# Values of the first attention branch made for four heads at a time, and a later place for the other branches' values

## The reference

```python
for l in range(2):
    h, hc = modulated rmsnorm of x, of ctx
    p = h @ w_in ; pc = hc @ w_in[:, :KV_COLS]      # latents, keys, values, queries, gates
    # branch 1 ("mla"): 8 heads, keys and values out of a latent of 256 features
    kv_m = (rmsnorm(ckv) * w) @ mla_w_ukv            # per head: 64 key, 64 value columns
    q_m  = (rmsnorm(cq) * w) @ mla_w_uq              # per head: 96 columns
    o_m  = softmax(q_m k_m^T * scale) v_m            # 512 queries on 768 keys
    # branch 2 ("swa"): window of 128 tokens and the context; branch 3 ("ax"): dense
    o_s, o_a likewise with k_s, v_s, k_a, v_a straight out of p
    x += gate * (sum over branches of sigmoid(g) * ((o * silu(z)) @ w_o)) @ w_out
    # in layer 0 the context takes the same way as queries; in layer 1 it doesn't
```

## Time and profile before

| | us |
|---|---|
| runs: median, lowest, highest | 1783.66, 1782.36, 1784.66 |
| span of the profiled execution | 1785.1 |
| TensorE busy | 1711.1 (96%) |
| VectorE busy | 1084.0 (61%) |
| ScalarE busy | 1049.3 (59%) |
| GpSimd busy | 528.0 (30%) |

### The profile page before, as it was taken

How to read it: one execution, slowest core, us unless ns; L and a number is a source line. 1 busy time by engine, 2 the same in 40 slices (tenths; PEclk the granted TensorE clock), 3 DMA queues, 4 the chain that set the end, 5 groups by cost and what they waited for, 6 DMA issues and landing times.

```text
span 1785.1 us, 27001 instructions
## 1 busy us (share of the span) xinstructions
PE 1711.1 (96%) x10554; PEld 1498.7 (84%) x10554; DVE 1084.0 (61%) x2185; ACT 1049.3 (59%) x1921; POOL 528.0 (30%) x300
## 2 busy tenths in 40 slices
PE   7999999999999999999999999999999999999997
PEld 3777888889989889899889996788888887888787
DVE  5543776765565566665775655477775756565634
ACT  3433778766666777666321253577776677786322
POOL 1523123222232212212322353322333432332442
PEclk9997999999999999999999999899999999999999
DMA  9111102111121111111644331111212221212642
GB/s 326 40 37 28 26 24 55 27 42 48 42 60 43 47 37 36 42 48 36 201 153 166 118 97 49 40 34 37 60 48 66 72 64 44 60 49 65 200 142 95
DMA packets 178527, 129.53 MB, mean 73 GB/s; under 512 B 21661, under 2 KB 167647, under 8 KB 178400
## 3 DMA queue, kind: packets, MB, share of 16 engines
q1 hardware_dynamic: 174242, 115.37, 22.7%
q10 hardware_dynamic: 2878, 8.24, 1.3%
q0 software_dynamic: 1280, 4.20, 0.7%
HBM read 123.58 MB, written 4.19 MB: 72 GB/s over the span
## 4 chain that ended last, share of the span: by engine, by line
PE 76%; DVE 10%; ACT 7%; issue 3%; POOL 2%; DMA 1%; SPq 0%; DVEq 0%; ACTq 0%; POOLq 0%
PE acc L1357 56%; PE wide L1415 6%; PE ptp L1435 6%; PE pv L1448 4%; PE pv L1449 3%; DVE nmax L1991 2%; ACT e L1682 2%; DVE pt L2016 1%; DMA w_raw<-in_ada_w 1%; POOL h_lo L1844 1%; DVE k_m L1552 1%; ACT w_hi L1600 1%; DVE k_s L1552 1%; DVE q_s L1552 1%; POOL w_lo L1806 1%
## 5 line engine op out<-in xcount | busy, mean ns | idle before, releaser
L1806 POOL TENSOR_TENSOR w_lo<-w_raw,w_hi 128x1024 fp32r<-128x1024 f32 (+2 forms) x192 | 392.0, 2045 | 1085.0 <-ACT w_hi L1600 1084.8
L1357 PE MATMUL acc<-h_hi,w_hi 128*128 128x512 f32 (+2 forms) x1320 | 463.3, 352 | 10.3 <-DVE cq_lo L1554 3.9
L1357 PE MATMUL acc<-h_hi,w_lo 128*128 128x512 f32 (+2 forms) x1320 | 462.0, 351 | 0.0
L1357 PE MATMUL acc<-h_lo,w_hi 128*128 128x512 f32 (+2 forms) x1320 | 457.7, 350 | 0.3 <-POOL h_lo L1844 0.3
L1991 DVE TENSOR_REDUCE nmax<-wide 128x1 f32<-128x768 f32 (+3 forms) x240 | 189.6, 790 | 167.9 <-PE wide L1415 166.2
L1357 PEld LDWEIGHTS acc<-h_hi,w_hi 128*128 128x128 f32 (+1 forms) x1320 | 248.4, 188 | 50.1 <-issue 7.9
L1697 ACT ACTIVATE pt<-ptp 128x512 fp32r<-128x512 f32 (+3 forms) x312 | 165.8, 563 | 210.4 <-PE ptp L1435 208.6
L1357 PEld LDWEIGHTS acc<-h_hi,w_lo 128*128 128x128 f32 (+1 forms) x1320 | 248.2, 188 | 33.4
L1357 PEld LDWEIGHTS acc<-h_lo,w_hi 128*128 128x128 f32 (+1 forms) x1320 | 246.1, 188 | 34.2 <-POOL h_lo L1844 0.5
L1689 ACT ACTIVATE e<-e,einv 128x768 f32<-128x768 f32 (+3 forms) x240 | 193.5, 806 | 70.2 <-DVE einv L2008 69.8
L2016 DVE TENSOR_TENSOR pt<-ptp,pt 128x512 fp32r<-128x512 f32 (+3 forms) x312 | 191.8, 640 | 43.9 <-ACT pt L1697 43.7
(11 more groups left out here) (216 smaller groups left out, 3103.1 us busy)
## 6 DMA issues: line engine op xcount, KB each, us to landing
w_raw<-in_w_in SPq DMA_DIRECT2D x102, 512.0 KB, 3.9
w_raw<-in_ada_w SPq DMA_DIRECT2D x48, 512.0 KB, 5.3
w_raw<-in_w_out SPq DMA_DIRECT2D x16, 512.0 KB, 4.2
w_raw<-in_w_in SPq DMA_DIRECT2D x16, 256.0 KB, 3.3
w_raw<-in_w_o_mla SPq DMA_DIRECT2D x16, 256.0 KB, 2.8
w_raw<-in_w_o_swa SPq DMA_DIRECT2D x16, 256.0 KB, 2.8
w_raw<-in_w_o_ax SPq DMA_DIRECT2D x16, 256.0 KB, 2.9
w_raw<-in_mla_w_uq SPq DMA_DIRECT2D x16, 144.0 KB, 2.4
```

The costliest lines, as they stand in the source:

```text
L1357: ins = nc.tensor.matmul(dst, lhs, rhs, start=first, stop=last)
L1806: nc.gpsimd.tensor_tensor(w_lo[s][:, 0:k], w_raw[s][:, 0:k], f(w_hi[s][:, 0:k]), ALU.subtract).then_inc(w_lo_ready, 1)
```

## The change

It does five things. `mla_head` makes values for four heads at once, at heads 0 and 4: three groups of two token tiles, each tile six matmuls with 256 moving columns. `v_m` becomes three separate places, used by pair number modulo three; the third lies at 12288 to 18432, in the first half of `v_s`. The chunks change with it: "mk" holds key columns of two heads and either value columns of four heads or the query columns of one; "mq" can hold the queries of two heads. An eviction of values is two pieces, one for each pair. And `values_a` may run only when the output of head 5 has been issued, which a new entry in `issued` tells; it also stands behind `values_b` in the queue now.

```diff
@@ attention, loop
                 O(turned)
+                if turned["closes"]:
+                    issued["o", turned["branch"], turned["h"]] = n["s"]
@@ mla_head
             if h % 2 == 0:
-                c = chunk("mk", l, h, h + 1 if h else 0)
+                four, heads = h % 4 == 0, (0, 1) if h == 0 else (h + 1,)
+                cq = chunk("mq", l, heads) if h == 0 else None
+                c = chunk("mk", l, h, None if four else h + 1)
...
-                vg = [group("vm", chunk_ids=(c,), mode="vm", l=l, cost=cost_of(128, 6 * 3), co=KKV * 2 * MLA_NOPE,
-                            tts=range(tt, tt + 3), what="vm", pair=h // 2, needs=lambda: latents) for tt in range(0, TT, 3)]
-                ready_v["mla", h // 2] = vg
-                qg = head_q(h + 1 if h else 0, c, KKV * 2 * (MLA_NOPE + MLA_V))
-            if h == 0 or h % 2 and h + 1 < HEADS:
-                qg += head_q(h + 1, chunk("mq", l, h + 1), 0)
-            if h % 2 == 0 and h:
-                return [s for g in (kg[0], vg[0], kg[1], vg[1], *qg) for s in g["steps"]]
-            return [s for g in qg + kg + vg for s in g["steps"]]
+                if four:
+                    vg = [group("vm", chunk_ids=(c,), mode="vm", l=l, cost=cost_of(256, 4 * 3), co=KKV * 2 * MLA_NOPE,
+                                tts=range(tt, tt + 2), what="vm", pair=h // 2, needs=lambda: latents) for tt in range(0, TT, 2)]
+                    ready_v["mla", h // 2] = ready_v["mla", h // 2 + 1] = vg
+                    cq = chunk("mq", l, heads) if cq is None else cq
+                    for i, hq in enumerate(heads):
+                        qg += head_q(hq, cq, i * KQ * MLA_K)
+                else:
+                    qg = head_q(h + 1, c, KKV * 2 * MLA_NOPE)
+            elif h + 1 < HEADS:
+                qg += head_q(h + 1, chunk("mq", l, (h + 1,)), 0)
+            if h == 0:
+                return [s for g in qg + kg + vg for s in g["steps"]]
+            if h % 4 == 0:
+                return [s for g in (kg[0], vg[0], kg[1], *vg[1:], *qg) for s in g["steps"]]
+            return [s for g in kg + qg for s in g["steps"]]
@@ queue
-        item("values_a", "mla", cost_of(256, 72), lambda s: ("mla", 1 + len(tgs)) in s, values_s(0))
         z_item(0, 3)
         item("values_b", "mla", cost_of(256, 72), lambda s: ("mla", 5) in s, values_s(TT // 2))
+        item("values_a", "mla", cost_of(256, 72), lambda s: ("o", "mla", 5) in s, values_s(0))
@@ memory
-    v_m = shared("v_m", [P, 2, TT, 2, 2, HD], R, 75776)
+    v_m = [shared(f"v_m{i}", [P, TT, 2, 2, HD], R, at) for i, at in enumerate((75776, 81920, 12288))]
@@ matmuls, mode "vm"
-                        c0 = g["co"] + k * 2 * MLA_V
-                        wv = [w[s][:, c0:c0 + 2 * MLA_V] for w in (w_hi, w_lo)]
+                        c0 = g["co"] + k * 4 * MLA_V
+                        wv = [w[s][:, c0:c0 + 4 * MLA_V] for w in (w_hi, w_lo)]
...
-                    run(a[:, i * 2 * HD:(i + 1) * 2 * HD], pairs)
+                    run(a[:, i * 4 * HD:(i + 1) * 4 * HD], pairs)
@@ pieces
+            if what == "vm":
...
+                for i in range(2):
+                    v = v_m[(g["pair"] + i) % 3][:, t0:t1]
+                    out_.append((v[:, :, :, 0, :], v[:, :, :, 1, :], got[:, :, 2 * i:2 * i + 2, :]))
```

More of the change, by code:

```diff
@@ L793, in schedule @@
             if h % 2 == 0:
-                cost += cost_of(SEQ, 6) + cost_of(CTX, 6) + 2 * cost_of(128, 18)
+                cost += cost_of(SEQ, 6) + cost_of(CTX, 6)
+            if h % 4 == 0:
+                cost += 3 * cost_of(256, 12)
             item(("mla", h), "mla", cost, lambda s, h=h: h < 2 or ("mla", h - 2) in s, lambda h=h: mla_head(h), urgent=True)
@@ L1094, in chunk_dma @@
                 got, at = [], 0
[L1095 to L1100, removed]
-                               t_in["mla_w_uq"][l, :, hq * MLA_K:(hq + 1) * MLA_K].rearrange("(k p) c -> p k c", p=P))]
+                for a, many in ((0, 2), (1, 4 if hq is None else 0)):
+                    for k in range(KKV if many else 0):
+                        rows = t_in["mla_w_ukv"][l, k * P:(k + 1) * P, h * P:(h + many) * P].rearrange("p (h a d) -> p h a d", h=many, a=2)
+                        got.append((raw[:, at:at + many * HD].rearrange("p (h d) -> p h d", h=many), rows[:, :, a, :]))
+                        at += many * HD
+                if hq is not None:
+                    got.append((raw[:, at:at + KQ * MLA_K].rearrange("p (k c) -> p k c", k=KQ),
+                                t_in["mla_w_uq"][l, :, hq * MLA_K:(hq + 1) * MLA_K].rearrange("(k p) c -> p k c", p=P)))
+                return got
             if kind == "mq":
-                hq = chunks[c][2]
-                return [(raw[:, 0:KQ * MLA_K].rearrange("p (k c) -> p k c", k=KQ),
-                         t_in["mla_w_uq"][l, :, hq * MLA_K:(hq + 1) * MLA_K].rearrange("(k p) c -> p k c", p=P))]
+                return [(raw[:, i * KQ * MLA_K:(i + 1) * KQ * MLA_K].rearrange("p (k c) -> p k c", k=KQ),
+                         t_in["mla_w_uq"][l, :, hq * MLA_K:(hq + 1) * MLA_K].rearrange("(k p) c -> p k c", p=P)) for i, hq in enumerate(chunks[c][2])]
             b, t = chunks[c][2:]
@@ L1115, in chunk_size @@
             if kind == "mk":
-                return KKV * 2 * (MLA_NOPE + MLA_V) + KQ * MLA_K
+                return KKV * 2 * MLA_NOPE + (KKV * 4 * MLA_V if chunks[c][3] is None else KQ * MLA_K)
             if kind == "mq":
-                return KQ * MLA_K
+                return len(chunks[c][2]) * KQ * MLA_K
             return KO * P if kind == "wo" else CHUNK
@@ L1192, in v_of @@
             if pa["branch"] == "mla":
-                v = v_m[:, (pa["h"] // 2) % 2, kt, pa["h"] % 2, :, :]
+                v = v_m[pa["h"] // 2 % 3][:, kt, pa["h"] % 2, :, :]
             else:
@@ L1526, in pieces @@
                 return out_ if only is None else out_[only:only + 1], w
-            if what in ("vs", "vm"):
+            if what == "vs":
                 t0, t1 = g["tts"][0], g["tts"][-1] + 1
-                heads = 2 * KVH if what == "vs" else 2
-                v = v_s[:, t0:t1] if what == "vs" else v_m[:, g["pair"] % 2, t0:t1]
-                got = src[:, 0:(t1 - t0) * heads * HD].rearrange("p (t g d) -> p t g d", g=heads, d=HD)
+                v = v_s[:, t0:t1]
+                got = src[:, 0:(t1 - t0) * 2 * KVH * HD].rearrange("p (t g d) -> p t g d", g=2 * KVH, d=HD)
                 return [(v[:, :, :, 0, :], v[:, :, :, 1, :], got)], None
+            if what == "vm":
+                t0, t1 = g["tts"][0], g["tts"][-1] + 1
+                got = src[:, 0:(t1 - t0) * 4 * HD].rearrange("p (t g d) -> p t g d", g=4, d=HD)
+                out_ = []
+                for i in range(2):
+                    v = v_m[(g["pair"] + i) % 3][:, t0:t1]
+                    out_.append((v[:, :, :, 0, :], v[:, :, :, 1, :], got[:, :, 2 * i:2 * i + 2, :]))
+                return out_, None
             raise KeyError(what)
```

## The result

The changed kernel takes 1799.45 us (median of 4 runs, 1797.22 to 1803.38), 1.0098 times the time before [1.0074, 1.0121]. Run again beside the kernel before it gave 1.0094 [1.0063, 1.0126]. It is **some 17 us slower**; forecast were 1778.8 us and a range to 1791. The profiled execution took 1798.48 us with a span of 1796.4.

The account below looks back on a forecast made before the run. The prediction took TensorE, busy for 96% of the span, to bound the kernel. Its terms, -15.4 - 5 - 1.8 + 18 - 3.7 + 3 = -4.9 us, taken off the median 1783.66, gave 1778.8 us, range 1766 to 1791.

Parts of the forecast that it names:

- The sign that the prediction had named: Prediction is wrong if branch 1's attentions, 196 and 162 us long before, are together shorter by over 10 us or longer at all.
- Term 1: Inside branch 1's attentions: 216 narrow value matmuls become 72 with 256 columns, 15.4 us less.
- Term 4: Units left without filling, mainly heads 4 and 5 of both layers, as values_a waits: 18 us more, bounds 9 and 24.
- Term 3: First filling of layer 1: the wait for the low part of its weights goes, 1.8 us less.
- Term 5: Heads 6 and 7: moved values thicken the filling and shrink the stops there, 3.7 us less, between 0 and 6.
- Term 6: Behind heads 4 and 5: two falls of the clock of 3.4 us, 3 us more, bounds 0 and 19.
- Term 2: 72 value matmuls ahead of the attentions: the low clock lasts shorter in each layer, 5 us less, bounds 0 and 7.8.
- the one on the clock: Rival: clock falls and stays down in heads 4 and 5, +18 or 19 us instead of +3, 1795 us; chance 0.16.

## Why the prediction was wrong

The sign that the prediction had named came true: branch 1's attentions are together 17.7 us longer, where it had allowed none. And heads 4 and 5 have six short falls of the clock, where it had allowed two.

**The premise failed first**: "what leaves TensorE's row of work shortens the kernel", read from 96% busy. Busy time says that TensorE works, not that it decides. Term 1's price per matmul was about right (0.108 and 0.118 us between starts over all rows at full clock), its sum of 15.4 us worked out rightly, and with everything else held in place the same amount brought nothing (+2.5 us [-0.9, +5.9]): 12.4 of the 15.8 us came back as stops. The prediction booked nothing against Term 1 itself. It booked stops in Term 4, nearly all of them for units that are left quite bare, and only 2.6 us for units that keep one step of filling.

**The step that is missing** is the wait for an accumulator: 9.8 us in the trace, 7 us in the runs by taking it out, 8 us by putting it in. The prediction listed what the moved groups compute and what they cost, and did not ask what they had separated. The values between the two key groups gave the evictions time; the earlier trace rows even had the first trace of it, 2.4 us of idle behind `k_m` in front of the values.

**Terms 3, 4 and 5** forecast 18 - 1.8 - 3.7 = 12.5 us more stops, pipeline included. TensorE's idle time in the attentions grew from 21.0 to 40.1 us; with 0.15 us of pipeline for each of 28 and 42 stops that is from 25.2 to 46.4 us, by 21.2. Of these 9.6 us are new waits for `k_m`, and 11.6 us are left, near the 12.5. The parts: without `k_m`, heads 4 and 5 are idle for 12.0 us more (Term 4), heads 6 and 7 for 5.5 us less (Term 5 said 3.7 with the pipeline), the wait for GpSimd has gone (Term 3), and heads 0 to 3 have 4.8 us more, where filling has become thinner.

**Term 6 was mis-sized**: +3 us for two short falls. There are five falls at bare units and two at the new wait, 27.3 us more at half clock within branch 1, which is 13 us by the slope of 0.48. Its reading that stops of 1.22 us were not followed by a fall holds for the earlier trace rows, but not for the stop of 1.17 us at 200.18 in the same trace. Over the runs Terms 2 and 6 together were forecast at -2 and are near +7 (15 us more at half clock). The rival that came nearest is the one on the clock (1795 us). It was given 0.16, for the reason that nothing fell in heads 4 and 5 before, which described the filling that the change takes away.

**Term 2 was right** in direction, and near in size: 5 us were forecast, the first exponential comes 6.3 us sooner in layer 0 of these two profiles, and in layer 1 10.2 us at half clock become 3.4. All 14 profiles of this study agree, with a first exponential at 169.6 us on average with narrow values and at 165.0 with wide ones. In the six with narrow values ahead of the attention of layer 0 there are 6.8 to 10.2 us at half clock between 145 and 165 us; in the eight with wide ones there are 0 or 3.4 us. Why the clock comes back sooner isn't shown.

As a sum in TensorE's row: -4.9 as forecast, +9.8 for the accumulator and +9 for the clock (from -2 to +7) is +14, of the 17 measured; 3 us stay unexplained. That the sum comes near with Term 1 left in it is no proof of Term 1: it counts the stops that came in its place beside it.

What stays open: how the clock decides was not tried, only what it did. That the low clock costs time, and does not only go with stops that cost it anyway, rests on the repeated matmuls and on the slope over the runs. Whether the third place could be had elsewhere, without late values, was not tried either.

## What to carry to other kernels

Before work is taken from the busiest engine, take it away alone (fewer products, nothing moved) and see whether the time follows; in a software pipeline filling may be what hides another engine's chain. When a group of instructions is moved, ask what it stood between: it may have been the distance that a buffer's eviction needed. And where the clock follows the work, a thin place costs its stops and then the slow stretch behind them, so even useless matmuls can pay there.

## What the hardware showed unexpectedly

The time of a run of one and the same kernel varies by over 15 us over 82 runs (1776.9 to 1792.5), and most of it goes with the clock: 1792.5 us at a mean of 0.977, 1777.8 at 0.986. The line through them leaves a spread of 1.3 us, of 3.6.

The same stop is followed by a fall of the clock in one execution and not in another. In head 6 of layer 0 TensorE waits 2.48 us for `pt` in the kernel before (until 330.85) and in the one with repeated matmuls in 6 places (until 329.54). The stretches behind it, in that order:

```profile
330.90:334.30 3.40, 3.40 (x22) 3.08 (x23) 2.24 (x5) 3.33 (x7) 0.00 (x0) 1.00 0.00 0
...
330.60:334.00 3.40, 3.40 (x15) 3.01 (x14) 2.69 (x7) 3.31 (x6) 0.00 (x0) 0.50 0.00 0
```

So the length of one stop does not tell whether the clock falls behind it.

Some instructions of VectorE are held up beside GpSimd. In the version with values of four heads only ahead of the attention, VectorE's subtraction of the query's low part took 2.86 us for 96x512, where ten others of its group of 16, with GpSimd idle, took 0.68, and GpSimd's split of weights ran over the same time:

```profile
235.93 2.86 DVE L1580 TENSOR_TENSOR q_m<-q_f,q_m 96x512 fp32r<-96x512 f32 x1
...
235.55 2.70 POOL L1834 TENSOR_TENSOR w_lo<-w_raw,w_hi 128x1024 fp32r<-128x1024 f32 x1 [1.23 <-ACT w_hi L1628]
```

The low part of `pt` behind it was late by that much, and TensorE stopped for 3.07 us. The kernel before has the same at another place:

```profile
1254.65 2.46 DVE L1552 TENSOR_TENSOR q_m<-q_f,q_m 96x512 fp32r<-96x512 f32 x1 [0.95 <-ACT q_m L1543]
...
1254.19 2.38 POOL L1806 TENSOR_TENSOR w_lo<-w_raw,w_hi 128x1024 fp32r<-128x1024 f32 x1 [0.20 <-ACT w_hi L1600]
```

The trace of the kernel before also tells which instructions are held. Every VectorE instruction that took over 1.3 times its usual time while `w_lo` was made reads two operands that both lie in SBUF: `y_lo<-y,y_hi` of 128x512 takes 2.21 us in 4 places beside `w_lo` and 0.69 in 9 away from it, `xres<-xres,x_add` of 128x256 1.68 us on average in 11 places and 0.43 in 29. Those that read an operand from PSUM are not held: `pt<-ptp,pt` of 128x512 takes 0.68 us in 32 places beside `w_lo`, as in 223 away from it. That is a comparison within one trace; no run moved the one away from the other.
